# Final rows of the last two expert blocks formed from PSUM; the final sum moved into the expert stage

## The reference

```
top_v, top_i = top_k(softmax(expert logits within the chosen group), 2)
gate         = group probability * top_v / sum(top_v)       # two gates per row
expert(x, e) = (silu(x @ w_gate[e]) * (x @ w_up[e])) @ w_down[e]
h            = h + gate[0] * expert(hn, e0) + gate[1] * expert(hn, e1)
y            = h * rsqrt(mean(h * h) + EPS) * norm_final_w
```

## Time and profile before

| | |
|---|---|
| median of 3 runs | 1506.64 us (1505.47 to 1507.14) |
| the profiled execution | 1505.11 us, span 1503.4 us |
| PE / DVE / ACT / POOL busy | 94% / 71% / 51% / 38% of the span |
| mean granted TensorE clock | 0.969 |
| moved | 361.07 MB; loads of `yy`: 8 of 1024.0 KB and one of 256 KB |

### The profile page before, as it was taken

One profiled execution on the slowest core, in us unless ns is written; L12 is line 12 of the kernel. 1 busy time (PEld: TensorE's weight loads), 2 busy tenths in 40 slices (PEclk: granted clock), 3 DMA queues, 4 the chain that ended last, 5 costly groups with the idle time before them and its releaser, 6 DMA issues. The chain is left out here.

```text
span 1503.4 us, 21686 instructions
## 1 busy us (share of the span) xinstructions
PE 1416.1 (94%) x7625; PEld 1233.0 (82%) x7625; DVE 1061.5 (71%) x1225; ACT 766.1 (51%) x891; POOL 568.4 (38%) x345
## 2 busy tenths in 40 slices
PE   6999999999999999899999659999999999999976
PEld 5999999999999998788877548888888888888852
DVE  6687722366666664545463579999999999999956
ACT  6332222333333335344433438777777777777734
POOL 2323324454444442485644014333433333333311
PEclk9999999999999999999999669999999999999997
DMA  5222333234444445876653659999999999999958
GB/s 197 65 78 86 126 95 111 80 130 143 144 141 147 138 144 167 294 219 239 209 168 130 231 201 383 402 396 390 377 381 362 389 379 383 385 388 387 369 211 343
DMA packets 115793, 361.07 MB, mean 240 GB/s; under 512 B 18772, under 2 KB 48468, under 8 KB 99348
## 3 DMA queue, kind: packets, MB, share of 16 engines
q1 hardware_dynamic: 100164, 322.37, 58.6%
q0 software_dynamic: 15568, 37.87, 7.3%
HBM read 316.52 MB, written 59.64 MB: 250 GB/s over the span
## 5 line engine op out<-in xcount | busy, mean ns | idle before, releaser
L2048 DVE TENSOR_TENSOR wgu_l<-wgu,wgu_h 128x2048 fp32r<-128x2048 f32 x128 | 290.0, 2288 | 27.4 <-ACT wgu_h L1928 26.5
L1928 ACT CAST wgu_h<-wgu 128x2048 fp32r<-128x2048 f32 x124 | 237.4, 1915 | 100.6 <-PE bank0and L64 100.5
L62 PE MATMUL bank0and<-wgu_h,xh_blk 128*128 128x512 f32 x512 | 203.7, 398 | 2.9 <-DVE xl_blk L2052 2.9
L64 PE MATMUL bank0and<-wgu_h,xl_blk 128*128 128x512 f32 x512 | 200.9, 392 | 0.0
L62 PE MATMUL bank0and<-xh,wh 128*128 128x352 f32 x576 | 197.6, 343 | 3.0 <-ACT raw L906 3.0
L63 PE MATMUL bank0and<-wgu_l,xh_blk 128*128 128x512 f32 x512 | 200.3, 391 | 0.0
L64 PE MATMUL bank0and<-xh,wl 128*128 128x352 f32 x576 | 186.7, 324 | 0.0
L63 PE MATMUL bank0and<-xl,wh 128*128 128x352 f32 x576 | 186.5, 324 | 0.0
L1671 POOL TENSOR_TENSOR wol<-wo,woh 128x1024 fp32r<-128x1024 f32 x48 | 121.4, 2536 | 123.5 <-ACT woh L996 123.5
L1835 POOL DMA_INDIRECT scratch_picked<-yb,dst x31 | 92.7, 2991 | 197.5 <-DVE yb L2042 197.5
L2057 DVE TENSOR_TENSOR wd_l<-wd,wd_h 128x1024 fp32r<-128x1024 f32 x128 | 148.2, 1219 | 1.2 <-ACT wd_h L1934 1.0
(11 more groups left out here) (496 smaller groups left out, 3234.5 us busy)
## 6 DMA issues: line engine op xcount, KB each, us to landing
wgu<-in_w_gate_up SPq DMA_DIRECT2D x128, 1024.0 KB, 7.6
wd<-in_w_down SPq DMA_DIRECT2D x128, 512.0 KB, 7.6
wo<-in_w_out SPq DMA_DIRECT2D x48, 512.0 KB, 4.9
w<-in_w_in_tiles SPq DMA_DIRECT2D x36, 512.0 KB, 3.6
yy<-scratch_picked SPq DMA_DIRECT2D x8, 1024.0 KB, 12.6
scratch_xb<-stage POOLq DMA_DIRECT2D x10, 512.0 KB, 4.0
xb<-scratch_xb SPq DMA_DIRECT2D x8, 640.0 KB, 4.4
scratch_uT<-feat SPq DMA_DIRECT2D x8, 528.0 KB, 5.0
```

The source lines that it names most:

```text
L62: nc.tensor.matmul(acc, lh, rh, start=start, stop=False)
L64: return nc.tensor.matmul(acc, ll, rh, start=False, stop=stop)
L1928: nc.scalar.copy(wgu_h[:, s], wgu[:, s]).then_inc(gu_high, 1)
L2048: nc.vector.tensor_tensor(wgu_l[:, s], wgu[:, s], wgu_h[:, s].bitcast(F32), ALU.subtract).then_inc(gu_split, 1)
```

## The change

- `combine` is gone as a block. Its work stands at the end of `experts`, on each engine behind the last expert block's own instructions, with no common start.
- Blocks 30 and 31 are no longer scattered to `picked`. Two extra tiles, 9 and 10, hold their final rows: `add_late` takes `h` of the block's rows, adds the gated row of the other expert (gathered from `picked`) and then the gated product straight from PSUM (banks 2 and 3, or 4 and 5), and ScalarE and VectorE normalise them like the others.
- A row with an expert in block 30 gets its final row from tile 9; one in block 31 from tile 10. So that no expert is missed where a row is in both, tile 9's sum is scattered back to `h` and tile 10 gathers `h` after it. GpSimd scatters zeros from `yb` to the rows of blocks 30 and 31 in `picked` at the start.
- All stores to the output go through an indirect DMA with a table of row numbers (`out_row`), in which the rows that belong to tile 9 or 10 are out of range. The two outputs are one, `y`.
- The loads of `yy` wait for `y_stored` at m * 16 + 32: the two scatters of zeros and those of blocks 0 to 29.
- `w_final` and tiles 0 to 3 of `h` are loaded ahead of the loop. The gates are stored to HBM and gathered back for the late rows.
- VectorE sums 8, 1, 0, 3; TensorE sums 2, 4, 5, 6, 7, in banks (0, 1), (6, 7), (2, 3), (0, 1), (6, 7). Its fourth waits for the normalisation of tile 2, its fifth for that of tile 4, and its third for the first late tile's sum, which reads banks 2 and 3.

Cut to its core:

```diff
-        of_row = own("of_row", [P, 2, MAXBLK], I32)
+        of_row = own("of_row", [P, 3, MAXBLK], I32)
...
+        h = [h_first[:, t, :] if t < FIRST else h_rest[:, t - FIRST, :] for t in range(NT + 1)]
+        h += [wgu[:, KT - 1].rearrange("p n f -> p (n f)"), wd[:, 1, :]]
+        other = [xg[:], wd[:, 0, :]]
+        total = [yb[:], h[NT + 2]]
...
+        def psum_of(t, half):
+            return bank[(0, 6, 2, 0, 6)[ON_PE.index(t)] + half][:, :]
...
+        def is_loaded(eng, t):
+            eng.wait_ge(h_loaded, 16 * (NT + 2))
+            eng.wait_ge(loaded[t], loaded_at[t])
...
+            sp.dma_start(S["gates"][0:SEQ, :].rearrange("(t p) k -> p t k", p=P), S["gate"][:, 0:NT, :]).then_inc(gates_stored, 16)
+            sp.dma_start(S["gates"][SEQ:T, :].rearrange("(t p) k -> p t k", p=TS), S["gate"][0:TS, NT:NT + 1, :]).then_inc(gates_stored, 16)
             m = blocks_but_three(sp) + 1
             load_gate_up(1)
+            sp.wait_ge(rows_ready, 1)
+            sp.dma_start(w_final[:], A["norm_final_w"][0].partition_broadcast(P)).then_inc(h_loaded, 16)
+            for t in range(FIRST):
+                sp.dma_start(h[t], S["h"][t * P:t * P + P, :]).then_inc(h_loaded, 16)
             with sp.Fori(0, m) as i:
                 load_gate_up(i + 2)
                 load_down(i + 1)
...
+            sp.wait_ge(gu_split, m * 4 + 8)
+            sp.sem_inc(holder, 1)
+            load_h(NT)
+            load_h(4)
             load_down(m + 1)
...
-                sp.dma_start(S["h_late"][0:rows_of(t), t - FIRST, :], S["h"][t * P:t * P + rows_of(t), :]).then_inc(S["final_loaded"][t], 16)
+            for t in (5, 6, 7):
+                load_h(t)
+            picked = S["picked"].rearrange("(k t) d -> t k d", k=2)
             sp.wait_ge(y_stored, m * 16 + 32)
+            for t in (8, 1, 0, 2, 3, 4, 5, 6, 7):
...
+                sp.sem_inc(holder, 1)
+                sp.dma_start(yy[t][0:live(t)], picked[t * P:t * P + live(t)]).then_inc(loaded[t], 16)
...
+            nc.gpsimd.memset(yb[:], 0.0).then_inc(zeroed, 1)
+            pool.wait_ge(zeroed, 2)
...
+            for j in range(2):
+                if j:
+                    pool.wait_ge(y_stored, 16)
+                then_own(pool, nc.gpsimd.tensor_copy(dst[:], of_row[:, 1, bass.ds(m + (1 + j), 1)]), index_copied, j + 2)
+                pool.indirect_dma_start(out=S["picked"], out_offset=bass.IndirectOffsetOnAxis(ap=dst[:], axis=0),
+                                        in_=yb[:], in_offset=None, bounds_check=2 * T - 1, oob_is_err=False).then_inc(y_stored, 16)
+            gather(2, 4)
...
+            scatter(m, m * 2 + 5)
+            pool.wait_ge(rows_ready, 2)
+            then_own(pool, nc.gpsimd.memset(late_gate[:], 0.0), zeroed, 3)
+            for j in range(2):
+                for k in range(3):
+                    nc.gpsimd.tensor_copy(late_row[:, j, k:k + 1], of_row[:, k, bass.ds(m + (1 + j), 1)]).then_inc(zeroed, 1)
+            pool.wait_ge(zeroed, 9)
+            pool.wait_ge(gates_stored, 32)
...
+            def store(n):
...
+                rows = out_row[0:r, t:t + 1] if t <= NT else late_row[:, t - NT - 1, 0:1]
+                pool.wait_ge(out_ready, n + 2)
+                landed = y_stored if t == NT + 1 else out_stored
+                pool.indirect_dma_start(out=A["y"], out_offset=bass.IndirectOffsetOnAxis(ap=rows, axis=0), in_=h[t][0:r, :],
+                                        in_offset=None, bounds_check=T - 1, oob_is_err=False).then_inc(landed, 16)
...
+            for j in range(2):
+                late_gather(j, late_gate[:, j, :], S["gates"])
+            late_gather(0, h[NT + 1], S["h"])
+            pool.wait_ge(xT_psum, m * 2 + 6)
+            pool.wait_ge(y_stored, m * 16 + 48)
+            pool.sem_inc(holder, 1)
+            late_gather(0, other[0], S["picked"], 2)
+            pool.wait_ge(down_split, m * 4 + 12)
+            pool.wait_ge(xg_loaded, m * 16 + 112)
+            pool.sem_inc(holder, 1)
+            late_gather(1, other[1], S["picked"], 2)
+            pool.wait_ge(h_loaded, 16 * (NT + 2))
+            pool.wait_ge(y_done, m + 2)
+            pool.sem_inc(holder, 1)
+            pool.indirect_dma_start(out=S["h"], out_offset=bass.IndirectOffsetOnAxis(ap=late_row[:, 0, 0:1], axis=0),
+                                    in_=total[0], in_offset=None, bounds_check=T - 1, oob_is_err=False).then_inc(y_stored, 16)
+            store(0)
+            pool.wait_ge(y_stored, m * 16 + 64)
+            pool.sem_inc(holder, 1)
+            late_gather(1, h[NT + 2], S["h"])
+            for n in range(1, NT + 3):
+                if ORDER[n] == NT + 2:
+                    pool.wait_ge(y_stored, m * 16 + 80)
+                    pool.sem_inc(holder, 1)
+                store(n)
+            pool.wait_ge(out_stored, 16 * (NT + 2))
...
+            for n, t in enumerate(ON_PE):
+                is_loaded(pe, t)
+                if n == 0:
+                    pe.wait_ge(diag_ready, 2 * len(ON_PE))
+                    pe.wait_ge(hT_done, m + 2)
+                if n == 2:
+                    pe.wait_ge(y_done, m + 1)
+                    pe.sem_inc(holder, 1)
+                if n > 2:
+                    pe.wait_ge(out_ready, ORDER.index(ON_PE[n - 3]) + 2)
+                for half in range(2):
+                    s = slice(half * 512, (half + 1) * 512)
+                    acc = psum_of(t, half)
+                    nc.tensor.matmul(acc, C["ident"][:], h[t][:, s], start=True, stop=False)
+                    nc.tensor.matmul(acc, diag[n // 2][:, n % 2, 0, :], yy[t][:, 0, s], start=False, stop=False)
+                    nc.tensor.matmul(acc, diag[n // 2][:, n % 2, 1, :], yy[t][:, 1, s], start=False, stop=True).then_inc(pe_summed, 1)
 
         @block.scalar
...
+            def add_late(j, loads):
+                dve.wait_ge(xg_loaded, m * 16 + loads)
+                dve.wait_ge(down_used, (m + j) * 4 + 4)
+                dve.sem_inc(holder, 1)
+                after(nc.vector.scalar_tensor_tensor(out=h[NT + 1 + j], in0=other[j], scalar=late_gate[:, j, 1:2], in1=h[NT + 1 + j],
+                                                     op0=ALU.mult, op1=ALU.add))
+                nc.vector.scalar_tensor_tensor(out=total[j], in0=(S["banks23"], S["banks45"])[j][:], scalar=late_gate[:, j, 0:1],
+                                               in1=h[NT + 1 + j], op0=ALU.mult, op1=ALU.add).then_inc(y_done, 1)
...
+            nc.vector.tensor_tensor(out_row[:], out_row_f[:], C["token_no"][:, :, 0], ALU.add).then_inc(out_ready, 1)
+            make_diag(0)
+            make_diag(1)
+            gated(m + 1)
+            low_down(m + 1, range(2))
+            low_hid(m + 1, (last_h, last_l))
+            dve.wait_ge(hT_psum, m + 2)
+            for n in range(2, len(ON_PE)):
+                make_diag(n)
+            low_down(m + 1, range(2, 4))
             add(NT)
+            dve.wait_ge(y_stored, m * 16 + 32)
+            dve.wait_ge(xg_loaded, m * 16 + 96)
+            dve.sem_inc(holder, 1)
...
+            add_late(0, 96)
+            add(1)
+            norm(NT)
+            norm(9)
             add(0)
...
+            norm(1)
+            norm(0)
+            norm(2)
+            add(3)
+            norm(4)
+            norm(3)
+            norm(5)
+            add_late(1, 128)
+            norm(6)
+            norm(10)
+            norm(7)
+
+
+FIRST = 4
+ON_PE = [2, 4, 5, 6, 7]
+ON_DVE = [8, 1, 0, 3]
+ORDER = [8, 9, 1, 0, 2, 4, 3, 5, 6, 10, 7]
```

More of the change, by code:

```diff
@@ new lines, in _ @@
+            gather(2, 4)
+            with pool.Fori(1, m + 1) as i:
+                gather(i + 2, i * 2 + 3)
+                scatter(i - 1, i * 2 + 4)
+            scatter(m, m * 2 + 5)
[4 more added lines that the diff above has]
+                    nc.gpsimd.tensor_copy(late_row[:, j, k:k + 1], of_row[:, k, bass.ds(m + (1 + j), 1)]).then_inc(zeroed, 1)
@@ L1968, in _, with after @@
             high_down(m + 1, range(2, 4))
+            act_own, links = S["act_own"]
+            def after(ins):
+                links[0] += 1
+                then_own(act, ins, act_own, links[0])
+            act.wait_ge(down_used, m * 4 + 4)
+            act.sem_inc(holder, 1)
+            for t in ORDER:
+                r = live(t)
+                if t in ON_PE:
+                    for half in range(2):
+                        act.wait_ge(pe_summed, 2 * ON_PE.index(t) + half + 1)
+                        after(nc.scalar.activation(junk[:, half * 512:(half + 1) * 512], psum_of(t, half), ACT.Square,
+                                                   accum_out=st[:, t, 2 * half:2 * half + 1]))
+                    after(nc.scalar.activation(st[:, t, 2:3], st[:, t, 2:3], ACT.Identity, bias=C["eps"][:], scale=1.0 / D))
+                    nc.scalar.activation(st[:, t, 1:2], st[:, t, 0:1], ACT.Sqrt, bias=st[:, t, 2:3], scale=1.0 / D).then_inc(rms, 1)
+                else:
+                    if t <= NT:
```

(31 more changed lines are left out.)

185 lines of the change are left out of this document (67 added, 118 removed).

## The result

| kernel | median, us | ratio to before, 95% interval |
|---|---|---|
| before | 1505.7 (20 runs) | |
| changed | 1507.6 (20 runs) | 1.0013 [1.0007, 1.0019] |

The prediction, 1500.2 in a range of 1496 to 1505, has the wrong sign. The profiled execution took 1507.17 us with a span of 1505.4 (before 1505.11 and 1503.4).

The account below looks back on a forecast made before the run. TensorE was taken to fill the expert loop, so the gain had to come from the tail: last store 1490.5 + 1.0 issue + 5.5 to the end = span 1497.0 against 1503.4; median 1500.2, range 1496 to 1505.

Parts of the forecast that it names:

- 5.5 us instead of 3.75 to the end: Kernel's end: from the last store's issue, now indirect, to the span's end takes 5.5 us, before 3.75.
- 5.5 us after the scatter's issue: Tail of before: the first `yy` load leaves 5.5 us after the last scatter's issue ended, taken as an undisturbed landing.
- the block's end that all engines shared also goes: Between experts and combining: the shared block end disappears; no size of its own was given.
- `yy` starts at 1447.0: Loads after block 29's scatter: first `yy` load at 1447.0 (1445.8 to 1447.9), 17.5 us earlier, taking 6.6 for the landing.
- TensorE starts at 1458.8: Tail: TensorE's first combining tile starts when `yy2` lands, taken as 11.8 us after the first load; clock fall counted.
- Rival 4: Tail, more gain: no clock fall (-2.4), stores ending after 3.75 (-1.75), start 1.2 sooner, down to 1495; chance 0.09.
- Sharing banks costs nothing: TensorE's tail: waits for shared banks cost 0, with 3.7 and 4.7 us of cover before the two waits.
- VectorE's 32.2 us: VectorE's tail: additions and normalisations of 31.2 us plus 1.0 for five gate operations, against 25.8 before.
- rival 1: Tail: GpSimd's issues bind at 2.82 us each, not the forecast mean 1.4; median 1510.7; chance 0.09.
- rival 2: Loop start: early loads starve TensorE, up to 3.4 us (1503.6), without cover 1509; forecast took 0; chance 0.10.
- The other additions there ... 0, at the most the length of two reciprocals, 0.4.: Loop start: second memset, two row-table operations and small gate stores cost 0, at most 0.4 us.
- rival 3: Tail does not start early: first late tile 5 us later (forecast 1460.3) pushes VectorE, giving 1505; chance 0.08.

Follow-up runs that it names:

- b_early_drain: Kernel before with one more GpSimd DRAIN behind the issue of block 30's scatter: 1507.64 us, 1.0016 of before.
- a_early_drain: Changed kernel with one more GpSimd DRAIN where it waits for the first late tile's sum: 1501.15 us, 0.9973 of before.
- a_loop_drain: Changed kernel with a GpSimd DRAIN in every expert-loop turn and SyncE, not GpSimd, waiting for the last stores: 1500.82 us, 0.9970 of before.
- a_kept_busy: Changed kernel with 24 unread products on TensorE between its last expert product and first combining tile: 1506.14 us, 1.0005 of before.
- c_all: Changed kernel with a_loop_drain's edits, yy loads ordered 8, 1, 2, 4, 0, 5, 3, 6, 7, a_memset_later's edit and 12 unread products: 1498.80 us, 0.9959 of before.
- a_memset_later: Changed kernel with the zeroing of the y buffer moved behind the issue of the first gather: 1506.00 us, 1.0004 of before.

## Why the prediction was wrong, step by step

Its forecast span was 1497.0, and 1505.4 came. Of the 8.4 us, 3.9 lie behind the last store's start and 4.5 ahead of it.

- **"5.5 us instead of 3.75 to the end": the step that failed.** From the end of the last issue it took 9.4 us (1495.96 to 1505.4): 2.3 until the store had landed and 0.2 until the drain began, 6.76 of drain and 0.2. The number came from a reading of before that was itself wrong: "5.5 us after the scatter's issue" was taken for a landing, though it ran up to the end of a block. b_early_drain takes it apart: 2.3 of landing, the rest drain. The prediction wrote "the block's end that all engines shared also goes" and gave that no price and no new place, and none of the four rivals had it. With the drain known, the same sum gives 1500.9 for the span. That is still 2.5 us faster than before, so the drain alone doesn't set the sign on paper; the 4.5 us ahead of the store, below, do the rest. In the runs the drain is enough: without most of it, and with the rest of the tail as it is, the kernel is 4 us (a_early_drain) to 4.5 us (a_loop_drain) faster than before.
- **`yy` starts at 1447.0.** It was 1449.21, above the bound of 1447.9: the scatter 1.1 later with the loop, and a landing of 7.8 us where 6.6 was taken; the upper bound, 7.53, was the like instruction.
- **TensorE starts at 1458.8.** It was 1463.27: 2.2 from the loads' start, 2.3 because the loads took 14.1 us and not 11.8. The fall of the clock was counted rightly (0.55, 0.50), its price somewhat too high: the first half tile took 4.51 us and not 5.25, which is why TensorE started 4.5 us late and ended 3.9 late. a_kept_busy shows that it could be had back only in part, since tile 4's load stood behind it. Rival 4's "no fall, -2.4" was therefore too large.
- **Sharing banks costs nothing.** Right: TensorE came to tiles 6 and 7 without a pause (1480.66). In c_all, with less cover, the wait appears: 0.32 us.
- **VectorE's 32.2 us.** Right: from 1456.88 to 1494.20 less 4.6 of waits is 32.7. TensorE set the end, also as forecast, 3.9 later (1491.12 for 1487.2); GpSimd took 0.8 and not 0.29 us to start the store behind VectorE.
- **GpSimd's issues, mean 1.4 (rival 1).** Right in that they don't bind: the eleven stores took 0.96 to 1.60 us each, 1.17 in the mean. They stood in a queue from 1475.61, and from the eighth on (1484.89) GpSimd waited for VectorE again.
- **Early loads cost 0 (rival 2).** ScalarE did wait for weights, 3.8 us over three copies between 910 and 930, and the DMA engines ran at 1.00 between 885 and 905 (before 0.83, 325 GB/s); but moving the loads back gave nothing that can be told. The value taken stands.
- **"The other additions there ... 0, at the most the length of two reciprocals, 0.4."** Too low: GpSimd's second memset held a VectorE operation for 0.68 us on the way to the first gather. The Trainium skill (SBUF — State Buffer, "SBUF: two separate sides") says that on the pair shared by VectorE and GpSimd one operation holds off another, and for which kinds: against a GpSimd operation that doesn't read SBUF, a VectorE operation in a 2-port mode; whichever starts first has the pair and "the other fully blocks". The prediction had set that aside from rows in which VectorE was not held by an issue; for the second memset the trace agrees with the rule: it ended at 864.68 and the held operation at 864.71, 0.86 us against 0.18; which mode it was in, no row says. Two VectorE operations beside the first memset were not held (0.46 and 0.45 us, as before). The time of the program doesn't show it (1.4 us in a_memset_later, within the uncertainty).
- **First late tile after 1463 (rival 3).** It ended at 1463.6, 3.3 late, but VectorE had 4.6 us of waits to take it up.

## What to carry to other kernels

When a block end is moved or taken out, price what closes it: ask the trace for the DRAIN of GpSimd at each block's end, count the DMAs it stands behind, and follow where that time goes. A gap between an engine's issue and the next block's first work is not a landing time until the closing instructions have been taken off. If GpSimd issues many DMAs, let it drain where it waits anyway and not right behind a DMA whose landing the next step needs early, and let another engine issue or wait for the last stores. And before moving one load forward, ask of the next one in the queue who waits for it.
